# A two-layer hybrid decoder step on eight cores: token blocks of 384, 384 and 272 columns in place of 512, 512 and 16

## The chip, the cores and the metric

One Trainium2 chip with two dies of four cores. The kernel runs on all 8 cores, each with its own eighth of the tokens and with no exchange between cores. The metric is the device time of the slowest core in microseconds (us). TensorE (PE) does the matmuls, ScalarE (ACT) and VectorE (DVE) take the results out of PSUM, GpSimd (POOL) issues the weight loads and SyncE (SP) the other transfers.

## What is computed

Two layers over a prompt group (8 sequences of 2048 positions, one on each core) and a sample group (128 sequences of one position, 16 on each core). Cut to what matters:

```python
proj = x @ w_in                                   # u | v | bg | cg | xb | xc | gates
vn = layer_norm(v);  ha = u * (tril(W_s) @ vn + b_s)      # branch A, chunks of 128 positions
z = cg * xb;         hb = bg * conv3(z)                   # branch B, causal, depthwise
hc = (window_means(xc) - xc) @ w_pool * pool_scale        # branch C
merged = sum_i sigmoid(gate_i) * (branch_i @ w_proj_i)
h = layer_norm(ALPHA * x + merged @ w_o)
out = layer_norm(ALPHA * h + relu(h @ w_ff1)**2 @ w_ff2)
```

The model width is 1024, the inner width of the last line 4096. The samples have the convolution's and the pooling's past as inputs, and a spatial matrix that is only its first diagonal entry, so in branches A and B their 16 columns need other constants and another source than the prompt columns.

## The kernel before, in words

Each core does its 2048 prompt tokens in two passes of 1024, per layer: four steps (layer 0 pass 0, layer 0 pass 1, layer 1 pass 0, layer 1 pass 1). The 16 sample tokens ride in the steps of pass 0, as tile 8 behind the eight prompt tiles of 128 tokens (`has_s`, `NTI = 9`). So the first and the third step hold 1040 tokens, the second and the fourth 1024.

Two kinds of products alternate. In one kind the tokens are stationary and the weights stream, 512 columns at a time, by tiles of 128 tokens (`xstat_project`: v, xc, w_o and w_ff2). In the other kind the weights are stationary, 128 by 128, and the tokens stream from `T`, or from the branch buffer `hv` (that is `B2`), in blocks of a table `WT`: 512, 512 and 16 columns in the steps with samples, 512 and 512 in the others. One output block (j, w) is a group of 8 matmuls into one PSUM bank. These block loops are

- branch A's u (per 128 channels c: a group of 8 for u, then one small matmul per token tile against the spatial matrix `WsT` or, for the samples, `WsS`, then on DVE a multiply-add and a multiply),
- branch B (`b_conv` and the loop over cp ahead of `conv_rows_out`): three groups per block (cg, xb, bg), ACT copies cg out, DVE multiplies by xb into `zbuf`, ACT does the first tap, DVE the other two and the multiply by bg. The samples have their own buffer `zsb`,
- `merge_branch`, three times: a gate group and a projection group per block, run with a lag of two blocks,
- `ff1_group`: one group, ReLU on ACT, multiply on DVE. For the first quarter (gq = 0) the order is by block w, outer, and j, inner, so that the first block starts while the layer norm still delivers the last tiles of `T` (`ln1.to_T`, a transpose on PE and a copy on ACT). For the other quarters j is outer.

The order on each engine is the order in which the program text adds the operations (`Sched.add`); each operation waits on semaphores for the writers and readers of its buffers. PSUM has 8 banks, taken by the one that was taken longest ago (`bank1`, `bank2`), ftmp has 6 buffers, zbuf 3. The ring of weights has 10 slots, filled by POOL in program order as the slots come free. The sample columns of `T` lie right behind the prompt columns (columns 1024 to 1039), so 1040 columns are contiguous.

Of the kernel before, what the change touches and what calls it, by code (L numbers as in the profile page):

```python
# [170 lines left out]
def build_nc():  # L171
# [454 lines left out]
    for kstep, (l, p) in enumerate(steps):  # L626
        nxt = steps[kstep + 1] if kstep + 1 < len(steps) else None
        has_s = (p == 0)
        NTI = 9 if has_s else 8
# [72 lines left out]
        for cp in range(4):  # L702
            if has_s and kstep > 0 and cp == 1:
                sample_rows()
            if has_s and kstep > 0 and cp == 2:
                sample_rows_out()
            su = load_unit(w_in[l, :, C_U + cp * 256: C_U + (cp + 1) * 256])
            for cc in range(2):
                c = cp * 2 + cc
                g = c // 2  # L710
                for w, (t0, n) in enumerate(cur["WT"]):
                    bu = bank1()
                    pe_group([(pcols(bu, 0, n), ring[:, su, kc, cc * 128:(cc + 1) * 128], T[:, kc, t0:t0 + n],
                               kc == 0, kc == 7) for kc in range(8)],
                             [slotb[su]] + [Tb[i] for i in wt_tiles(w)], [bank[bu]])
# [2 lines left out]
                    if w < 2:
                        pe_group([(pcols(bs_, j * 128, 128), xh[:, 4 * w + j, c * 128:(c + 1) * 128],
                                   WsT[:, g, :], True, True) for j in range(4)],  # L720
                                 [XH[4 * w + j] for j in range(4)] + [lcst], [bank[bs_]])
                        dve_stt(ftmp[:, f, :].rearrange("p (j t) -> p j t", j=4),
                                pcols(bs_, 0, 512).rearrange("p (j t) -> p j t", j=4),
                                pv(l, PV_LNVG, c),
                                Bias2[:, c:c + 1, :].to_broadcast([128, 4, 128]),
                                ALU.mult, ALU.add, [bank[bs_], lcst, cst], [ftb[f]])
                    else:
                        pe_group([(pcols(bs_, 0, SP_), xh[:, 8, c * 128:(c + 1) * 128],
                                   WsS[:, g, :], True, True)], [XH[8], lcst], [bank[bs_]])
                        dve_stt(ftmp[:, f, 0:SP_], pcols(bs_, 0, SP_), pv(l, PV_LNVG, c),  # L730
                                Bias2s[:, c:c + 1].to_broadcast([128, SP_]),
                                ALU.mult, ALU.add, [bank[bs_], lcst, cst], [ftb[f]])
# [20 lines left out]

        for cp in range(4):
# [8 lines left out]
            for cc in range(2):  # L763
                c = cp * 2 + cc
                prev_z = None
                for w, (t0, n) in enumerate(cur["WT"]):
# [11 lines left out]
                    if w < 2:
                        zi = state["zb"] % 3
                        state["zb"] += 1  # L780
                        dve_tt(zbuf[:, zi, 2:2 + n], ftmp[:, f, 0:n], pcols(bxb, 0, n), ALU.mult,
                               [ftb[f], bank[bxb]], [zbb[zi]])
                        if w == 0:
                            if p == 0:
                                S.add("dve", lambda e, zi=zi: e.memset(zbuf[:, zi, 0:2], 0.0), (), [zbb[zi]])
                            else:
                                dve_copy(zbuf[:, zi, 0:2], zcar[:, c, :], [zcb], [zbb[zi]])
                        else:
                            dve_copy(zbuf[:, zi, 0:2], zbuf[:, prev_z, 512:514], [zbb[prev_z]], [zbb[zi]])
                            if p == 0:  # L790
                                dve_copy(zcar[:, c, :], zbuf[:, zi, 512:514], [zbb[zi]], [zcb])
                            else:
                                dve_copy(zsf[:, c, SP_:SP_ + 2], zbuf[:, zi, 512:514], [zbb[zi]], [zsfb])
                        prev_z = zi
                        item = (c, w, t0, n, (lambda k3, zi=zi, n=n: zbuf[:, zi, k3:k3 + n]), zbb[zi], f, bbg)
                    else:
                        dve_tt(zsb[:, c, :, 2], ftmp[:, f, 0:n], pcols(bxb, 0, n), ALU.mult,
                               [ftb[f], bank[bxb]], [zsbb])
# [310 lines left out]
```

How the kernel before makes its waits and increments, by code:

```python
        def run(engname, e):  # L100
            known = {}
            for op in sched.ops[engname]:
                deps = {}
                for k, v in op.raw.items():
                    if k == engname and engname == "pe":
                        continue
                    deps[k] = max(deps.get(k, -1), v)
                for k, v in op.other.items():
                    if k == engname:
                        continue
                    deps[k] = max(deps.get(k, -1), v)
                for k, v in deps.items():
                    if known.get(k, -1) >= v:
                        continue
                    e.wait_ge(sems[k], v)
                    known[k] = v
                ins = op.emit(e)
                if op.dma:
                    ins.then_inc(sems[op.tok[0]], 16)
                else:
                    ins.then_inc(sems[op.tok[0]], 1)
            if engname == "sp":
                for k, v in final_waits.items():
                    if known.get(k, -1) < v:
                        e.wait_ge(sems[k], v)
```

## Time and profile before

| | us |
|---|---|
| median of 3 runs (lowest to highest) | 2671.63 (2668.45 to 2672.88) |
| the profiled execution, its own time | 2672.26 |
| its span, slowest core (the eight: 2662.4 to 2670.7) | 2670.7 |
| PE busy, share of the span | 2564.7, 96% |
| DVE busy | 1201.4, 45% |
| ACT busy | 777.5, 29% |
| mean granted clock of PE on the eight cores | 0.986 to 0.989 |

The profile is of core 3, the slowest. Busy time is summed over the instructions of an engine; matmuls overlap, so a matmul's own duration is longer than the distance to the next one. Idle time of an engine stands with what ended it. The granted clock is a share of 2.4 GHz, and 0.5 of it is 1.2 GHz.

### The profile page before, as it was taken

The numbers are of one execution on the slowest core, as the hardware profiler recorded it, in microseconds if no ns is written. First come the engines' busy times: TensorE is split into PE (matmuls) and PEld (weight loads), VectorE is DVE, ScalarE is ACT, GpSimd is POOL, SyncE is SP. The second block draws the span as 40 slices with busy tenths as digits, with TensorE's granted clock in tenths as the row PEclk, the third lists the DMA queues.
The fourth block names the chain that finished last, engine by engine and source line by source line (L and its number), as shares of the span: only waits on it lengthen the run. The fifth ranks groups of instructions, "written<-read, shape, count | busy, mean of one in ns | idle before, by whom it ended". The sixth has DMA issues, their size and how long they took to land.

```text
span 2670.7 us, 40806 instructions; the slowest of 8 cores (2662.4 to 2670.7 us)
## 1 busy us (share of the span) xinstructions
PE 2564.7 (96%) x14756; PEld 1245.5 (47%) x14756; DVE 1201.4 (45%) x2135; ACT 777.5 (29%) x1471; POOL 266.1 (10%) x320
## 2 busy tenths in 40 slices
PE   6699999899999999999999999989999999999997
PEld 3344454444444445444445445544444444544443
DVE  2526415533572631643374452273337444146336
ACT  2122252411321215421151223351114122524112
POOL 1111000010011110111011100101001111000000
PEclk9799999999999999999999999999999999999999
DMA  8755545474695563559577463544747764464442
GB/s 152 127 71 65 75 61 72 60 99 64 123 172 70 74 86 43 76 69 127 80 179 108 62 87 49 82 62 72 103 73 169 92 80 68 58 87 67 63 69 74
DMA packets 312952, 231.81 MB, mean 87 GB/s; under 512 B 7602, under 2 KB 298674, under 8 KB 312724
## 3 DMA queue, kind: packets, MB, share of 16 engines
q0 software_dynamic: 299968, 186.26, 52.9%
q1 hardware_dynamic: 12788, 42.94, 5.0%
q8 instruction: 123, 2.02, 0.3%
q14 instruction: 73, 0.60, 0.1%
HBM read 397.51 MB, written 19.87 MB: 156 GB/s over the span
## 4 chain that ended last, share of the span: by engine, by line
PE 84%; DVE 7%; issue 4%; DMA 3%; ACT 2%; DVEq 0%; SPq 0%; ACTq 0%; POOLq 0%
PE ps L342 83%; DVE R L379 2%; DVE R L376 2%; DMA ring<-w_ff 1%; ACT T L362 1%; PE ps L350 1%; DMA R<-x_p 1%; DVE mv L371 0%; ACT B L362 0%; DMA maskt<-c_mask 0%; DVE sm L369 0%; DVE stat L646 0%; ACT sm L362 0%; DVE stat L647 0%; ACT xctm L362 0%
## 5 line engine op out<-in xcount | busy, mean ns | idle before, releaser
L342 PE MATMUL ps<-T,ring 128*128 128x512 bf16 (+1 forms) x7040 | 1314.6, 339 | 10.2 <-ACT T L362 8.6
L342 PEld LDWEIGHTS ps<-T,ring 128*128 128x128 bf16 x7040 | 591.6, 98 | 668.1 <-issue 27.7
L362 ACT ACTIVATE ftmp<-ps 128x512 f32<-128x512 f32 (+1 forms) x640 | 317.0, 513 | 1225.0 <-PE ps L342 1221.6
L342 PE MATMUL ps<-ring,B 128*128 128x512 bf16 x2720 | 598.6, 380 | 8.8 <-DVE sm L491 3.7
L365 DVE TENSOR_TENSOR B<-ftmp,ps 128x512 bf16<-128x512 f32 (+1 forms) x560 | 321.4, 583 | 480.7 <-ACT ftmp L362 278.7
L342 PEld LDWEIGHTS ps<-ring,B 128*128 128x128 bf16 x2720 | 263.4, 98 | 322.4 <-issue 16.2
L342 PE MATMUL ps<-B,ring 128*128 128x512 bf16 (+1 forms) x1920 | 375.4, 337 | 0.0
L365 DVE TENSOR_TENSOR ftmp<-ftmp,ps 128x512 f32<-128x512 f32 x160 | 93.4, 584 | 434.4 <-PE ps L342 434.4
L342 PEld LDWEIGHTS ps<-B,ring 128*128 128x128 bf16 x1920 | 163.0, 97 | 181.5
L342 PE MATMUL ps<-ring,T 128*128 128x512 bf16 x1088 | 241.5, 379 | 3.1 <-DVE mv L648 2.6
L321 POOL DMA_DIRECT2D ring<-w_in x128 | 112.7, 883 | 872.5 <-PE ps L342 841.2
L321 POOL DMA_DIRECT2D ring<-w_ff x96 | 84.2, 881 | 900.9 <-PE ps L342 728.1
L342 PEld LDWEIGHTS ps<-ring,T 128*128 128x128 bf16 x1088 | 105.0, 98 | 124.2 <-issue 4.5
L362 ACT ACTIVATE xctm<-R 128x1024 bf16<-128x1024 f32 x102 | 107.8, 1057 | 152.2 <-DVE sm L491 77.3
L365 DVE TENSOR_TENSOR R<-R,ps 128x1024 f32<-128x1024 f32 x68 | 83.0, 1221 | 153.3 <-PE ps L342 153.3
L379 DVE SCALAR_TENSOR_TENSOR ftmp<-zbuf,pvec_sb,ftmp 128x512 f32<-128x512 f32 x128 | 96.1, 751 | 62.6 <-ACT ftmp L362 55.6
L365 DVE TENSOR_TENSOR B<-B,ftmp 128x512 bf16<-128x512 bf16 x160 | 94.2, 589 | 17.2 <-DVE ftmp L365 0.7
L379 DVE SCALAR_TENSOR_TENSOR R<-stage,sm,lnbc_sb 128x1024 f32<-128x1024 f32 x68 | 87.3, 1284 | 7.8 <-DVE sm L491 0.9
L379 DVE SCALAR_TENSOR_TENSOR stage<-R,sm,lnbc_sb 128x1024 f32<-128x1024 f32 x68 | 87.3, 1284 | 7.8 <-DVE mv L371 1.6
L362 ACT ACTIVATE ftmp<-zbuf,pvec_sb 128x512 f32<-128x512 f32 x64 | 52.0, 813 | 127.5 <-DVE zbuf L383 104.7
L379 DVE SCALAR_TENSOR_TENSOR R<-R,ps 128x1024 f32<-128x1024 f32 x34 | 41.5, 1221 | 79.4 <-PE ps L342 79.4
L362 ACT ACTIVATE B<-ps,pvec_sb 128x128 bf16<-128x128 f32 (+1 forms) x272 | 72.5, 420 | 0.6 <-issue 0.6
(89 smaller groups left out, 972.0 us busy)
## 6 DMA issues: line engine op xcount, KB each, us to landing
ring<-w_in POOLq DMA_DIRECT2D x112, 512.0 KB, 8.6
ring<-w_ff POOLq DMA_DIRECT2D x64, 512.0 KB, 13.3
ring<-w_ff POOLq DMA_DIRECT2D x32, 1024.0 KB, 10.6
ring<-w_in POOLq DMA_DIRECT2D x16, 1024.0 KB, 10.1
hx<-R SPq DMA_DIRECT2D x17, 512.0 KB, 5.4
R<-hx SPq DMA_DIRECT2D x17, 512.0 KB, 4.8
R<-x_p SPq DMA_DIRECT2D x16, 512.0 KB, 13.0
ring<-w_proj_a POOLq DMA_DIRECT2D x16, 512.0 KB, 16.0
```

What stands on the lines that cost most here:

```text
L321: return S.add("pool", lambda e: e.dma_start(out=out, in_=in_), reads, writes, dma=True)
L342: ins = e.matmul(o, l, r, start=st, stop=sp_)
L350: ins = e.transpose(o, i, idn)
L362: return S.add("act", lambda e: e.activation(out=out, in_=in_, func=func, **kw), reads, writes)
L365: return S.add("dve", lambda e: e.tensor_tensor(out=out, in0=in0, in1=in1, op=op), reads, writes)
L376: return S.add("dve", lambda e: e.scalar_tensor_tensor(out=out, in0=in0, scalar=scalar, in1=in1, op0=op0, op1=op1, accum_out=accum_out), r ...
L379: return S.add("dve", lambda e: e.scalar_tensor_tensor(out=out, in0=in0, scalar=scalar, in1=in1, op0=op0, op1=op1), reads, writes)
```

## The change

The block table of the steps with samples becomes (0, 384), (384, 384), (768, 272), and the last block now has two prompt tiles (256 columns) and the samples (16 columns). The other steps keep 512 and 512. The code that told prompt from samples by the block's number now splits inside a block; `wt_tiles` and a new `w_of` give the tiles of a block and the block of a tile. In the start of the first quarter of w_ff1, the groups with j = 3 to 6 now stand ahead of the last `ln1.to_T` in steps with samples, where it was j = 3 and 4; in the other steps nothing moves.

```diff
-WT = [(0, 512), (512, 512), (PT, SP_)]
+WT_S = [(0, 384), (384, 384), (768, 256 + SP_)]
+WT_P = [(0, 512), (512, 512)]
...
     def wt_tiles(w):
-        return list(range(4 * w, 4 * w + 4)) if w < 2 else [8]
+        if cur["NTI"] == 9:
+            return list(range(3 * w, 3 * w + 3))
+        return list(range(4 * w, 4 * w + 4))
+
+    def w_of(i):
+        return i // 3 if cur["NTI"] == 9 else i // 4
...
-        cur["NTI"], cur["WT"] = NTI, (WT if has_s else WT[:2])
+        cur["NTI"], cur["WT"] = NTI, (WT_S if has_s else WT_P)
...
+                    tl = wt_tiles(w)
+                    np128 = len([i for i in tl if i < 8])
+                    mms = [(pcols(bs_, (i - tl[0]) * 128, 128), xh[:, i, c * 128:(c + 1) * 128], WsT[:, g, :],
+                            True, True) for i in tl if i < 8]
+                    if 8 in tl:
+                        mms.append((pcols(bs_, np128 * 128, SP_), xh[:, 8, c * 128:(c + 1) * 128], WsS[:, g, :],
+                                    True, True))
+                    pe_group(mms, [XH[i] for i in tl] + [lcst], [bank[bs_]])
...
+                    if 8 in tl:
+                        dve_stt(ftmp[:, f, np128 * 128:np128 * 128 + SP_], pcols(bs_, np128 * 128, SP_),
+                                pv(l, PV_LNVG, c), Bias2s[:, c:c + 1].to_broadcast([128, SP_]),
                                 ALU.mult, ALU.add, [bank[bs_], lcst, cst], [ftb[f]])
...
+        def b_conv(c, w, t0, n, parts, f, bbg):
+            for (a0, m, zsrc, zb_) in parts:
+                fa = ftmp[:, f, a0:a0 + m]
+                act(fa, zsrc(0), AF.Identity, [zb_, cst], [ftb[f]], bias=pv(l, PV_CB, c), scale=pv(l, PV_CW0, c))
+                for k3 in (1, 2):
+                    dve_stt(fa, zsrc(k3), pv(l, PV_CW0 + k3, c), fa, ALU.mult, ALU.add,
+                            [zb_, ftb[f], cst], [ftb[f]])
+            dve_tt(hv[:, c, t0:t0 + n], ftmp[:, f, 0:n], pcols(bbg, 0, n), ALU.mult,
+                   [ftb[f], bank[bbg]], [HB[(c, w)]])
...
+                    m = min(n, PT - t0)
...
+                    parts = [(0, m, (lambda k3, zi=zi, m=m: zbuf[:, zi, k3:k3 + m]), zbb[zi])]
+                    if m < n:
+                        dve_tt(zsb[:, c, :, 2], ftmp[:, f, m:n], pcols(bxb, m, n - m), ALU.mult,
                                [ftb[f], bank[bxb]], [zsbb])
                         dve_copy(zsf[:, c, 0:SP_], zsb[:, c, :, 2], [zsbb], [zsfb])
+                        parts.append((m, SP_, (lambda k3, c=c: zsb[:, c, :, k3]), zsbb))
+                    b_conv(c, w, t0, n, parts, f, bbg)
...
-        ff1_group(0, 3, 0, AG)
-        ff1_group(0, 4, 0, AG)
+        n1 = 7 if has_s else 5
+        for j in range(3, n1):
+            ff1_group(0, j, 0, AG)
         ln1.to_T(last)
-        for j in range(5, 8):
+        for j in range(n1, 8):
             ff1_group(0, j, 0, AG)
```

Where the order moves, in three places.

TensorE in the first `merge_branch` of the first step, before (`T,ring` is a gate group, `B,ring` a projection group):

```order
L342 MATMUL ps<-B,ring 128x512 x8
L342 MATMUL ps<-T,ring 128x512 x8
L342 MATMUL ps<-B,ring 128x512 x8
L342 MATMUL ps<-T,ring 128x512 x8
L342 MATMUL ps<-B,ring 128x16 x8
L342 MATMUL ps<-T,ring 128x16 x8
```

And now:

```order
L344 MATMUL ps<-B,ring 128x384 x8
L344 MATMUL ps<-T,ring 128x384 x8
L344 MATMUL ps<-B,ring 128x384 x8
L344 MATMUL ps<-T,ring 128x384 x8
L344 MATMUL ps<-B,ring 128x272 x8
L344 MATMUL ps<-T,ring 128x272 x8
```

The number and the order of the groups stay, only their widths move; the same holds for branch B and the later quarters of w_ff1.

VectorE in branch B of the first step, one c (128 channels), before:

```order
L365 TENSOR_TENSOR zbuf<-ftmp,ps 128x512
L785 MEMSET zbuf 128x2
L379 SCALAR_TENSOR_TENSOR ftmp<-zbuf,pvec_sb,ftmp 128x512 x2
L365 TENSOR_TENSOR B<-ftmp,ps 128x512
L365 TENSOR_TENSOR zbuf<-ftmp,ps 128x512
L383 COPY zbuf<-zbuf 128x2
L383 COPY zcar<-zbuf 128x2
L379 SCALAR_TENSOR_TENSOR ftmp<-zbuf,pvec_sb,ftmp 128x512 x2
L365 TENSOR_TENSOR B<-ftmp,ps 128x512
L365 TENSOR_TENSOR zsb<-ftmp,ps 128x16
L383 COPY zsf<-zsb 128x16
L379 SCALAR_TENSOR_TENSOR ftmp<-zsb,pvec_sb,ftmp 128x16 x2
```

And now, its third block alone:

```order
L367 TENSOR_TENSOR zbuf<-ftmp,ps 128x256
L385 COPY zbuf<-zbuf 128x2
L385 COPY zcar<-zbuf 128x2
L367 TENSOR_TENSOR zsb<-ftmp,ps 128x16
L385 COPY zsf<-zsb 128x16
L381 SCALAR_TENSOR_TENSOR ftmp<-zbuf,pvec_sb,ftmp 128x256 x2
L381 SCALAR_TENSOR_TENSOR ftmp<-zsb,pvec_sb,ftmp 128x16 x2
L367 TENSOR_TENSOR B<-ftmp,ps 128x272
```

The third block now has a prompt part and a sample part, four instructions more on DVE per c (the multiply into zbuf, the copy of the two columns before it, two taps) and one more on ACT.

TensorE at the start of the first quarter of w_ff1 in the first step (`identb,xctm` are the transposes of `ln1.to_T`, the last of them tile 8), before:

```order
L342 MATMUL ps<-T,ring 128x512 x8
L350 MATMUL ps<-identb,xctm 128x128 x8
L342 MATMUL ps<-T,ring 128x512 x16
L350 MATMUL ps<-identb,xctm 128x128 x8
L342 MATMUL ps<-T,ring 128x512 x16
L350 MATMUL ps<-identb,xctm 128x128 x8
L342 MATMUL ps<-T,ring 128x512 x88
L342 MATMUL ps<-T,ring 128x16 x64
```

And now:

```order
L344 MATMUL ps<-T,ring 128x384 x8
L352 MATMUL ps<-identb,xctm 128x128 x8
L344 MATMUL ps<-T,ring 128x384 x16
L352 MATMUL ps<-identb,xctm 128x128 x8
L344 MATMUL ps<-T,ring 128x384 x32
L352 MATMUL ps<-identb,xctm 128x128 x8
L344 MATMUL ps<-T,ring 128x384 x72
L344 MATMUL ps<-T,ring 128x272 x64
```

Two more groups stand ahead of the last transposes, and the 64 matmuls of the last block are 272 wide.

## Rows read from the trace of the kernel before

**Rows 1.** The page's head and its first part.
```profile
span 2670.7 us, 40806 instructions; the slowest of 8 cores (2662.4 to 2670.7 us)
PE 2564.7 (96%) x14756; PEld 1245.5 (47%) x14756; DVE 1201.4 (45%) x2135; ACT 777.5 (29%) x1471; POOL 266.1 (10%) x320
```
**Rows 2.** Groups by shape, matmuls and weight loads: count, busy us, mean ns, idle before.
```profile
L342 PE MATMUL ps<-T,ring 128*128 128x512 bf16 x5632 | 1281.7, 382 | 9.6 <-ACT T L362 8.6 <-DVE ftmp L379 0.9
...
L342 PE MATMUL ps<-T,ring 128*128 128x16 bf16 x1408 | 54.6, 169 | 0.7 <-DVE B L365 0.7
...
L350 PE MATMUL ps<-identb,xctm 128*128 128x128 bf16 x272 | 21.6, 224 | 11.1 <-ACT xctm L362 11.1
...
L342 PE MATMUL ps<-B,ring 128*128 128x16 bf16 x384 | 16.7, 169 | 0.0
```
**Rows 3.** Timeline, PE, a merge of step 1: start, duration, what, [idle before].
```profile
395.28 0.35 PE L342 MATMUL ps<-B,ring 128*128 128x16 bf16 x8
395.69 1.89 PE L342 MATMUL ps<-B,ring 128*128 128x512 bf16 x8
...
402.59 0.35 PE L342 MATMUL ps<-B,ring 128*128 128x16 bf16 x8
```
**Rows 4.** Groups by shape, DVE and ACT in the block loops.
```profile
L365 DVE TENSOR_TENSOR B<-ftmp,ps 128x512 bf16<-128x512 f32 x448 | 307.5, 687 | 458.7 <-ACT ftmp L362 278.5 <-PE ps L342 160.2 <-DVE ftmp L379 12.8
...
L379 DVE SCALAR_TENSOR_TENSOR ftmp<-zbuf,pvec_sb,ftmp 128x512 f32<-128x512 f32 x128 | 96.1, 751 | 62.6 <-ACT ftmp L362 55.6 <-DVE ftmp L379 0.5
...
L362 ACT ACTIVATE ftmp<-zbuf,pvec_sb 128x512 f32<-128x512 f32 x64 | 52.0, 813 | 127.5 <-DVE zbuf L383 104.7 <-DVE zbuf L785 22.7
...
L365 DVE TENSOR_TENSOR B<-ftmp,ps 128x16 bf16<-128x16 f32 x112 | 18.2, 167 | 22.0 <-PE ps L342 19.9 <-ACT ftmp L362 0.2
...
L379 DVE SCALAR_TENSOR_TENSOR ftmp<-zsb,pvec_sb,ftmp 128x16 f32<-128x16 f32 x32 | 7.5, 235 | 5.7 <-ACT ftmp L362 3.9 <-DVE ftmp L379 0.2
...
L362 ACT ACTIVATE ftmp<-zsb,pvec_sb 128x16 f32<-128x16 f32 x16 | 6.5, 407 | 37.5 <-DVE zsb L365 37.5
```
**Rows 5.** Timeline, DVE, one c of branch B in step 3.
```profile
1558.14 0.69 DVE L365 TENSOR_TENSOR zbuf<-ftmp,ps 128x512 f32<-128x512 f32 x1
...
1563.24 0.69 DVE L365 TENSOR_TENSOR zbuf<-ftmp,ps 128x512 f32<-128x512 f32 x1 [0.91 <-PE ps L342]
...
1567.40 0.17 DVE L365 TENSOR_TENSOR zsb<-ftmp,ps 128x16 f32<-128x16 f32 x1
...
1568.18 0.58 DVE L379 SCALAR_TENSOR_TENSOR ftmp<-zsb,pvec_sb,ftmp 128x16 f32<-128x16 f32 x2 [0.33 <-ACT ftmp L362]
...
1569.11 0.69 DVE L365 TENSOR_TENSOR zbuf<-ftmp,ps 128x512 f32<-128x512 f32 x1
```
**Rows 6.** Timeline, PE, start of the first quarter of w_ff1 in step 1.
```profile
478.83 1.89 PE L342 MATMUL ps<-T,ring 128*128 128x512 bf16 x8
...
482.27 0.61 PE L350 MATMUL ps<-identb,xctm 128*128 128x128 bf16 x8 [1.55 <-ACT xctm L362]
...
486.65 0.61 PE L350 MATMUL ps<-identb,xctm 128*128 128x128 bf16 x8 [0.32 <-ACT xctm L362]
487.09 3.62 PE L342 MATMUL ps<-T,ring 128*128 128x512 bf16 x16
494.55 0.61 PE L350 MATMUL ps<-identb,xctm 128*128 128x128 bf16 x8 [3.84 <-ACT xctm L362]
```
**Rows 7.** Timeline, PE, end of that quarter.
```profile
517.59 0.34 PE L342 MATMUL ps<-T,ring 128*128 128x16 bf16 x8 [0.37 <-DVE B L365]
518.23 2.38 PE L342 MATMUL ps<-ring,B 128*128 128x512 bf16 x7 [0.30 <-DVE B L365]
```
**Rows 8.** Windows: busy of PE, PEld, DVE, ACT, POOL, then granted clock, DMA share, GB/s.
```profile
494.50:500.00 5.50, 5.45 (x24) 2.45 (x25) 2.66 (x4) 3.79 (x6) 0.00 (x0) 0.69 0.52 70
518.20:525.00 6.80, 6.77 (x24) 2.81 (x25) 1.43 (x3) 0.07 (x1) 1.20 (x2) 0.75 0.89 82
1794.50:1800.00 5.50, 5.48 (x24) 2.47 (x25) 2.66 (x4) 3.77 (x6) 0.00 (x0) 0.69 0.02 4
```

More of the change, by code:

```diff
@@ L717, in build_nc @@
                     f = ft_next()
[L718 to L731, printed above, removed]
+                    tl = wt_tiles(w)
[6 more added lines that the diff above has]
+                    pe_group(mms, [XH[i] for i in tl] + [lcst], [bank[bs_]])
+                    dve_stt(ftmp[:, f, 0:np128 * 128].rearrange("p (j t) -> p j t", j=np128),
+                            pcols(bs_, 0, np128 * 128).rearrange("p (j t) -> p j t", j=np128),
+                            pv(l, PV_LNVG, c),
+                            Bias2[:, c:c + 1, :].to_broadcast([128, np128, 128]),
+                            ALU.mult, ALU.add, [bank[bs_], lcst, cst], [ftb[f]])
+                    if 8 in tl:
+                        dve_stt(ftmp[:, f, np128 * 128:np128 * 128 + SP_], pcols(bs_, np128 * 128, SP_),
+                                pv(l, PV_LNVG, c), Bias2s[:, c:c + 1].to_broadcast([128, SP_]),
                                 ALU.mult, ALU.add, [bank[bs_], lcst, cst], [ftb[f]])
@@ L777, in build_nc @@
                     act(ftmp[:, f, 0:n], pcols(bcg, 0, n), AF.Copy, [bank[bcg]], [ftb[f]])
[L778 to L787, printed above, removed]
-                        else:
[L789 to L797, printed above, removed]
@@ new lines, in build_nc @@
+                    m = min(n, PT - t0)
+                    zi = state["zb"] % 3
+                    state["zb"] += 1
+                    dve_tt(zbuf[:, zi, 2:2 + m], ftmp[:, f, 0:m], pcols(bxb, 0, m), ALU.mult,
+                           [ftb[f], bank[bxb]], [zbb[zi]])
+                    if w > 0:
+                        zp, mp = prev_z
+                        dve_copy(zbuf[:, zi, 0:2], zbuf[:, zp, mp:mp + 2], [zbb[zp]], [zbb[zi]])
+                    elif p == 0:
+                        S.add("dve", lambda e, zi=zi: e.memset(zbuf[:, zi, 0:2], 0.0), (), [zbb[zi]])
+                    else:
+                        dve_copy(zbuf[:, zi, 0:2], zcar[:, c, :], [zcb], [zbb[zi]])
@@ new lines, in build_nc @@
+                    if t0 + m == PT:
+                        if p == 0:
+                            dve_copy(zcar[:, c, :], zbuf[:, zi, m:m + 2], [zbb[zi]], [zcb])
+                        else:
+                            dve_copy(zsf[:, c, SP_:SP_ + 2], zbuf[:, zi, m:m + 2], [zbb[zi]], [zsfb])
+                    prev_z = (zi, m)
+                    parts = [(0, m, (lambda k3, zi=zi, m=m: zbuf[:, zi, k3:k3 + m]), zbb[zi])]
+                    if m < n:
+                        dve_tt(zsb[:, c, :, 2], ftmp[:, f, m:n], pcols(bxb, m, n - m), ALU.mult,
@@ L902, in c_lin @@
             pe_group(mms, [Dtb[di], slotb[swp]], [bank[bh], bank[bh + 1]])
-            w = i // 4 if i < NT128 else 2
+            w = w_of(i)
             for dj in range(8):
@@ L915, in wo @@
             c0, n = tile_cols(i)
-            w = i // 4 if i < NT128 else 2
+            w = w_of(i)
             b = xstat_project(i, wslots, [MG[(j, w)] for j in range(8)], lambda kc, c0=c0: mg[:, kc, c0:c0 + 128])
@@ L1000, in ff2 @@
                 c0, n = tile_cols(i)
-                w = i // 4 if i < NT128 else 2
+                w = w_of(i)
                 b = xstat_project(i, slots, [AG[(j, w)] for j in range(8)], lambda kc, c0=c0: av[:, kc, c0:c0 + 128])
```

11 lines of the change are left out of this document (1 added, 10 removed).

## The prediction

> **What bounds the kernel now.** I read the page's head first: TensorE is busy for 96% of the span, VectorE for 45% [rows 1], so what a change is worth is what it takes from TensorE's own row of matmuls, unless it makes TensorE wait. Then the groups by shape: the 512-column matmuls carry the time and hardly wait (9.6 us of idle ahead of 5632 of them), and there are 1408 + 384 = 1792 matmuls of 16 columns in the two steps with samples [rows 2]. Then TensorE's timeline in a merge, for the distance between matmuls, since a matmul's own duration (382 ns, 169 ns) overlaps the next: two groups of 16-column matmuls take 395.69 - 395.28 = 0.41 us, that is about 25.2 ns a matmul with the shared drain left out, and the whole cycle of six groups takes 402.59 - 395.28 = 7.31 us [rows 3]. Last, the places in which the 1040-column blocks meet a wait: branch B on VectorE [rows 5] and the start and end of the first quarter of w_ff1 [rows 6 to 8].
>
> **Term 1, the matmuls.** Their number stays (three groups of 8 per block row, before and after), their columns too (1040). Only widths move. The cycle of 7.31 us holds 32 matmuls of 512 and 16 of 16 columns: (7310 - 16 x 25.2) / 32 = 215.9 ns for 512. For 128 columns, a burst of eight takes 0.61 us [rows 6] with 224 ns for the last one [rows 2]: (610 - 224) / 7 = 55.1 ns. Between them lies a line of (215.9 - 55.1) / 384 = 0.419 ns a column with 1.5 ns to spare at zero, which is 2.4 GHz. The 16-column matmul would cost 8 ns on it and costs 25: that is the waste. Neither 384 nor 272 columns occur in the trace. Bounds: from below the line, 162.3 and 115.4 ns; it is interpolation between two measured widths, and at 128 columns nothing else shows. Then three matmuls cost 2 x 162.3 + 115.4 = 440.0 ns, where they cost 2 x 215.9 + 25.2 = 457.0 ns, 17.0 ns less; times 1792 it is **30.4 us**. With the 55.1 ns wrong by 1 ns it is 29 to 32. From above: a straight line through 16 and 512 columns (0.384 ns a column), which gives 166.6 and 123.5 ns and a sum of 457, nothing gained. I take the line through 128, for it is the nearer width to 272 and it alone agrees with the slope of 2.4 GHz.
>
> The Trainium skill ("TensorE: Matmul & The Clock Gate", section "Back-to-back issue gap") speaks against this change: in a real stream of weight loads and matmuls it gives some 81 ns at 128 columns and some 131 ns at 512, and by any such single line three matmuls with 1040 columns cost the same however they are split, so term 1 would be zero. The trace does not agree (55.1 and 215.9 ns). The same section's table also has a least distance of about 25 ns for small matmuls, and there the trace agrees (25.2 ns).
>
> **Term 2, the start and the end of the first quarter of w_ff1 (twice).** TensorE waits there for the layer norm's last tile: 1.55, 0.32 and 3.84 us [rows 6]. That chain (w_o result, norm and transposes through VectorE and ScalarE) doesn't depend on the blocks, but two ReLUs and two multiplies of the first groups stand in it in order; each is 128 columns shorter, about 0.11 us on ScalarE and 0.13 us on VectorE (1.05 ns a column [rows 4]), together 0.48 us, so the last transposes can start at 494.07 and not 494.55. By then TensorE has done five groups of 1.727 us (8.63 us) before, and now seven of 1.298 us (9.09 us): 0.46 us more. So 0.94 us a step; the three waits become about 1.98, 1.2 and 1.8 us. At the end the 64 matmuls of 16 columns go faster than ScalarE and VectorE can empty the banks, which costs 0.37 + 0.30 us [rows 7] plus drains, about 0.75 us; with 272 columns a group takes 0.92 us and its two readers about 0.4 us each, so that goes. (0.94 + 0.75) x 2 = **3.4 us**.
>
> **Term 3, the clock.** After the 3.84 us wait the granted clock is 0.69 over 5.5 us, in both steps, and after the small matmuls of the first step 0.75 over 6.8 us [rows 8]; full speed is 1.0, the dips go to 1.2 GHz. Each costs (1 - 0.69) x 5.5 = 1.7 us. The third has no more small matmuls ahead of it. The first two follow a wait that is halved to 1.8 us; the wait of 1.55 us [rows 6] was followed by no dip. I take all three as gone, **5.2 us**, and from 1.7 us as the other bound; dips elsewhere may come or go by 1.7 us each.
>
> **Term 4, VectorE in branch B: nothing, but with thin cover.** One c takes 1569.11 - 1558.14 = 10.97 us, in which VectorE waits for TensorE only once, 0.91 us [rows 5]; the rest, 10.06 us, is one chain of its own work and ScalarE's tap in the middle. Per column the chain costs two multiplies (1.05 ns each), two taps (1.04) and ScalarE's tap (0.82) [rows 4], 5.0 ns, and the columns stay 1040. A prompt block of 512 takes 1567.40 - 1563.24 = 4.16 us [rows 5], so 4.16 - 2.56 = 1.60 us of it are fixed. The third block now has a prompt part: plus 1.60 us fixed. Of the sample part some 0.6 us are saved, since its first multiply and copy run under ScalarE's prompt tap and its last multiply joins the 272-wide one. The sample tap on ScalarE waits for VectorE's prompt taps (same ftmp buffer) and stays exposed. So the chain is about **11.1 us** per c, against 3 x (16 x 162.3 + 8 x 115.4) = 10.56 us on TensorE: VectorE becomes the slower one in this loop and falls behind by 0.5 us per c, 4.3 us over eight. What hides it is the eight banks: a group waits for the reader of the eighth group before it, that is, the second group of a block waits for the end of the chain three blocks earlier. For the last block that comes at 10.56 x 7 + 7.79 + 0.92 = 82.6 us after the loop's start, and the chain of three blocks before ends at 2.6 + 0.5 + 7 x 11.1 = 80.8 us. Cover 1.8 us. Behind the loop, the projection of the third block needs the last result: seven groups, 84.5 + 8.7 = 93.2 us, against 91.9. Cover 1.3 us. The backlog is then worked off in the merge, where VectorE needs about 3.1 us in 7.
>
> **The rest costs nothing.** The u loop gets one more VectorE instruction of about 0.2 us per c: some 3.5 of 4.0 us, hidden. The other loops have the same instructions on 1040 columns. POOL and SP issue the same transfers in the same order; TensorE waits for none of them behind the first 100 us, and they are asked for at a 3.5% faster pace in half of the program. The steps without samples don't change.
>
> **Sum.** 30.4 + 3.4 + 5.2 = 39.0 us from the execution's own 2672.26 us is 2633.3 us. The median of the runs stands 0.6 us below that execution; so **2633 us**, 1.4% less.
>
> **The rivals.**
> - *Branch B becomes bound by VectorE's chain.* Same place, but the banks don't hold the lag, because the chain is longer than 11.1 us or the lag starts earlier. For it: cover of under 2 us on an estimate of eight instructions. Against: only the excess beyond the cover counts. If the loop ran wholly at 11.1 us it would give back 16 x 0.54 = 8.6 us: 2642 us; at 11.4 us, 13.4 us: 2646 us.
> - *The dips of the clock stay* or others come: 3.5 us back, 2636.5 us; two more elsewhere, 2640 us.
> - *A fixed cost at any width* (the line through 16 and 512 columns): term 1 is zero and the sum is 2672.3 - 8.6 = 2663.7 us, with the dips kept 2668 or so, within 0.2%. Against it stand the 55.1 ns at 128. The skill's rule of a single line, above, is this case.
> - *Slower: the weight load shows.* A load lasts about 98 ns and a 512-column matmul covers it amply; under 272 columns (115 ns) the cover is thin. If each matmul behind a 272-wide one were held up by 25.2 ns, the least distance seen, it would be 1792 x 25.2 = 45.2 us: 2633 + 45 = 2678 us, slower. It decides from (39.0 - 5.3) / 1792 = 19 ns on for less than 0.2% gain, from 22 ns for a loss. Against: at 16 and at 128 columns, with the same loads, the distances are 25 and 55 ns.
> - *The change doesn't do what it says*: the order shows 384 and 272 columns on every block loop, so no.
>
> **Numbers.** A measurement of this kernel can tell about 0.2% (5.3 us) from no change. Chances: the forecast with its dips either way (2628 to 2640) 0.76, branch B bound 0.16, fixed cost at any width 0.03 (half of it within 0.2%), slower 0.02, faster than 2628 0.03. The range from 2627 to 2647 us leaves out some 0.1. Faster by over 0.2%: 0.96; within 0.2%: 0.02; slower: 0.02.
>
> **What would show it.** Merges: a cycle of six groups in 7.04 us in place of 7.31; matmuls of 384 and 272 columns 162 and 115 ns apart. Branch B: VectorE without a wait for TensorE, blocks three per 11.1 us, TensorE at 10.56 us per c with at most a short wait at the last c; if TensorE waits for VectorE there in many places, the first rival holds. First quarter of w_ff1: last wait about 1.8 us, no idle of TensorE at its end, granted clock 1.0 behind both. It is wrong if the cycle of a merge isn't below 7.2 us.

## The result, and the profile after

The changed kernel takes 2635.7 us, median of 17 runs (the kernel before, in the same rounds: 2672.4 us), a ratio of 0.9872 with a 95% interval of 0.9849 to 0.9894: 1.3% less. The forecast was 2633 us in a range from 2627 to 2647 us. Ratios, and the times given for the runs below, leave out the runs in which the cores of one die or of both had a lower granted clock, but the ratio above still holds three of the changed kernel, at 2656 to 2660 us with cores 4 and 5 at a clock of 0.978, and without them it is 0.986, 1.4% less.

The page's head of the changed kernel, and its first part (core 1, the slowest):

```profile
span 2632.7 us, 40970 instructions; the slowest of 8 cores (2627.3 to 2632.7 us)
...
PE 2529.3 (96%) x14756; PEld 1373.7 (52%) x14756; DVE 1214.5 (46%) x2215; ACT 791.8 (30%) x1487; POOL 266.3 (10%) x320
```

TensorE has the same 14756 matmuls as in [rows 1] and is busy for 35.4 us less; the span is 38.0 us shorter. VectorE has 80 instructions more and ScalarE 16.

Groups by shape, which answer to [rows 2] (count, busy us, mean ns of one, idle before):

```profile
L344 PE MATMUL ps<-T,ring 128*128 128x384 bf16 x2816 | 491.6, 327 | 1.4 <-DVE B L367 1.0
...
L344 PE MATMUL ps<-T,ring 128*128 128x272 bf16 x1408 | 184.9, 279 | 1.9 <-DVE B L367 1.3 <-ACT B L364 0.7
```

TensorE's timeline in a merge of the first step, which answers to [rows 3] (start, duration, what):

```profile
396.42 1.09 PE L344 MATMUL ps<-B,ring 128*128 128x272 bf16 x8
...
398.27 1.46 PE L344 MATMUL ps<-B,ring 128*128 128x384 bf16 x8
399.57 1.46 PE L344 MATMUL ps<-T,ring 128*128 128x384 bf16 x8
...
403.47 1.09 PE L344 MATMUL ps<-B,ring 128*128 128x272 bf16 x8
```

The cycle of six groups is 403.47 - 396.42 = 7.05 us, where it was 7.31 us. A matmul of 384 columns stands (399.57 - 398.27) / 8 = 162.5 ns from the next, one of 272 columns (398.27 - 396.42) / 16 = 115.6 ns.

VectorE's timeline in branch B, one c of the third step, which answers to [rows 5]:

```profile
1482.72 0.55 DVE L367 TENSOR_TENSOR zbuf<-ftmp,ps 128x384 f32<-128x384 f32 x1
...
1486.19 0.55 DVE L367 TENSOR_TENSOR zbuf<-ftmp,ps 128x384 f32<-128x384 f32 x1
...
1489.71 0.41 DVE L367 TENSOR_TENSOR zbuf<-ftmp,ps 128x256 f32<-128x256 f32 x1
...
1491.54 1.07 DVE L381 SCALAR_TENSOR_TENSOR ftmp<-zbuf,pvec_sb,ftmp 128x256 f32<-128x256 f32 x2 [0.52 <-ACT ftmp L364]
1493.22 0.57 DVE L381 SCALAR_TENSOR_TENSOR ftmp<-zsb,pvec_sb,ftmp 128x16 f32<-128x16 f32 x2 [0.61 <-ACT ftmp L364]
...
1494.32 0.55 DVE L367 TENSOR_TENSOR zbuf<-ftmp,ps 128x384 f32<-128x384 f32 x1
```

In this c no instruction waits for TensorE any more; apart from waits of 0.17 us behind VectorE's own taps, all are for ScalarE's tap. One c takes 1494.32 - 1482.72 = 11.60 us, more than TensorE's 10.56. Over the loop the c differ: 11.4 us in the shortest, 11.8 us in the longest, 11.6 us in the mean of both steps. And TensorE now waits for VectorE at the end of this loop. Its timeline at the end of branch B in the third step:

```profile
1540.58 11.05 PE L344 MATMUL ps<-T,ring 128*128 128x272 bf16 x72 [0.21 <-DVE B L367]
1551.99 3.31 PE L344 MATMUL ps<-T,ring 128*128 128x272 bf16 x24 [0.36 <-DVE B L367]
1555.46 2.39 PE L344 MATMUL ps<-T,ring 128*128 128x384 bf16 x16 [0.15 <-DVE B L367]
...
1563.41 1.09 PE L344 MATMUL ps<-B,ring 128*128 128x272 bf16 x8 [0.36 <-DVE B L367]
```

That is 1.08 us in the step, 0.36 us of it in the merge behind the loop; the first step has 1.04 us.

TensorE's timeline at the start of the first quarter of w_ff1 in the first step, which answers to [rows 6], and its end, which answers to [rows 7]:

```profile
472.62 1.46 PE L344 MATMUL ps<-T,ring 128*128 128x384 bf16 x8
475.71 0.61 PE L352 MATMUL ps<-identb,xctm 128*128 128x128 bf16 x8 [1.63 <-ACT xctm L364]
...
480.09 0.61 PE L352 MATMUL ps<-identb,xctm 128*128 128x128 bf16 x8 [1.17 <-ACT xctm L364]
480.54 5.36 PE L344 MATMUL ps<-T,ring 128*128 128x384 bf16 x32
487.52 0.61 PE L352 MATMUL ps<-identb,xctm 128*128 128x128 bf16 x8 [1.62 <-ACT xctm L364]
487.96 19.28 PE L344 MATMUL ps<-T,ring 128*128 128x384 bf16 x136
507.08 13.11 PE L344 MATMUL ps<-ring,B 128*128 128x512 bf16 x60
```

The waits are 1.63, 1.17 and 1.62 us (1.55, 0.32 and 3.84 before), there is no wait at the end, and from the first group to w_ff2 it takes 507.08 - 472.62 = 34.46 us (39.40 before). The windows behind these two places and behind the same start in the third step, which answer to [rows 8] (busy of PE, PEld, DVE, ACT, POOL, then granted clock, DMA share, GB/s):

```profile
487.50:493.00 5.50, 5.48 (x39) 3.50 (x40) 3.68 (x8) 4.88 (x10) 0.00 (x0) 1.00 0.26 36
505.50:512.00 6.50, 6.50 (x39) 3.58 (x37) 2.62 (x5) 1.19 (x3) 0.88 (x1) 1.00 1.17 129
1766.80:1772.30 5.50, 5.46 (x39) 3.51 (x40) 3.67 (x8) 4.89 (x10) 0.00 (x0) 1.00 0.12 16
```

The granted clock is 1.00 in all three, where it was 0.69, 0.75 and 0.69. Over the eight cores the mean granted clock rose from 0.986 to 0.989 before to 0.988 to 0.990.

### The profile page after: what moved, and what is told of

Its sections match the earlier page's. It is cut to its first block, busy times and chain, and to the rows that moved or that the text cites. A ratio compares the mean times of both kernels' runs of the same rounds, so it can differ in the third digit from the quotient of the medians.

```text
span 2632.7 us, 40970 instructions; the slowest of 8 cores (2627.3 to 2632.7 us)
## 1 busy us (share of the span) xinstructions
PE 2529.3 (96%) x14756; PEld 1373.7 (52%) x14756; DVE 1214.5 (46%) x2215; ACT 791.8 (30%) x1487; POOL 266.3 (10%) x320
## 4 chain that ended last, share of the span: by engine, by line
PE 83%; DVE 8%; issue 4%; ACT 3%; DMA 1%; DVEq 0%; SPq 0%; ACTq 0%
PE ps L344 82%; DVE R L381 2%; DVE R L378 2%; DVE ftmp L381 1%; ACT T L364 1%; PE ps L352 1%; ACT ftmp L364 1%; DMA R<-x_p 1%; DVE mv L373 0%; ACT B L364 0%; DVE zbuf L367 0%; DVE sm L371 0%; DMA maskt<-c_mask 0%; DVEq L116 0%; DVE stat L652 0%
## 5 line engine op out<-in xcount | busy, mean ns | idle before, releaser
L344 PE MATMUL ps<-T,ring 128*128 128x384 bf16 (+2 forms) x7040 | 1289.4, 339 | 12.0 <-ACT T L364 8.6
L344 PEld LDWEIGHTS ps<-T,ring 128*128 128x128 bf16 x7040 | 685.4, 98 | 544.5 <-issue 23.1
L364 ACT ACTIVATE ftmp<-ps 128x384 f32<-128x384 f32 (+2 forms) x640 | 327.5, 517 | 1145.3 <-PE ps L344 794.3
L367 DVE TENSOR_TENSOR B<-ftmp,ps 128x512 bf16<-128x512 f32 (+2 forms) x560 | 326.4, 584 | 458.1 <-ACT ftmp L364 256.9
L344 PE MATMUL ps<-B,ring 128*128 128x384 bf16 (+2 forms) x1920 | 370.3, 338 | 0.7 <-DVE B L367 0.7
L367 DVE TENSOR_TENSOR ftmp<-ftmp,ps 128x384 f32<-128x384 f32 (+1 forms) x160 | 93.5, 584 | 413.5 <-PE ps L344 413.2
L344 PEld LDWEIGHTS ps<-B,ring 128*128 128x128 bf16 x1920 | 187.7, 98 | 148.4 <-issue 1.4
L381 DVE SCALAR_TENSOR_TENSOR ftmp<-zbuf,pvec_sb,ftmp 128x384 f32<-128x384 f32 (+2 forms) x160 | 103.2, 645 | 73.4 <-ACT ftmp L364 65.1
L364 ACT ACTIVATE ftmp<-zbuf,pvec_sb 128x384 f32<-128x384 f32 (+2 forms) x80 | 58.5, 731 | 176.9 <-DVE zbuf L385 110.5
L367 DVE TENSOR_TENSOR B<-B,ftmp 128x384 bf16<-128x384 bf16 (+1 forms) x160 | 94.2, 589 | 16.7
```

Source lines behind the costliest of these rows:

```text
L344: ins = e.matmul(o, l, r, start=st, stop=sp_)
L364: return S.add("act", lambda e: e.activation(out=out, in_=in_, func=func, **kw), reads, writes)
L367: return S.add("dve", lambda e: e.tensor_tensor(out=out, in0=in0, in1=in1, op=op), reads, writes)
L381: return S.add("dve", lambda e: e.scalar_tensor_tensor(out=out, in0=in0, scalar=scalar, in1=in1, op0=op0, op1=op1), reads, writes)
```

## Experiments

Each ran beside the kernel before. "The changed kernel" is 2635 us in a second set of runs too:

> The changed kernel once more, as the yardstick on the same chip as the next three: 2635.7 us, 0.986 to 0.987 of the kernel before.

Measured: 0.9862 (0.9845 to 0.988) of the kernel before, 2634.7 us.

**The price of a 16-column matmul, by leaving them out.**

```diff
     def pe_group(mms, reads, writes):
+        if len(mms) == 8 and mms[0][2].shape[-1] == SP_ and mms[-1][4] and not mms[0][4]:
+            mms = [mms[0][:4] + (True,)]
```

> The kernel before; each group of eight 16-column matmuls is cut to its first one, so the sample columns get only an eighth of their sums in u, branch B, the gates, the projections and w_ff1. It leaves out 7/8 of 1792 = 1568 matmuls. Theory (25.2 ns each): 39.5 us less, 2633 us, some 1 to 3 us lower if the waits and the dip at the end of the first quarter go too. Rival, that a 16-column matmul costs the 8 ns of the line through 128 and 512 columns: 12.5 us less, 2660 us.

Measured: 0.9884 (0.9866 to 0.9902), 2642 us, so 31 us less and not 39.5. TensorE's timeline in a merge of this run:

```profile
387.98 0.17 PE L344 MATMUL ps<-B,ring 128*128 128x16 bf16 x1
388.01 0.17 PE L344 MATMUL ps<-T,ring 128*128 128x16 bf16 x1
388.03 1.89 PE L344 MATMUL ps<-B,ring 128*128 128x512 bf16 x8
...
394.94 0.17 PE L344 MATMUL ps<-B,ring 128*128 128x16 bf16 x1
```

The cycle is 394.94 - 387.98 = 6.96 us against 7.31 us, 0.35 us for 14 matmuls left out, 25 ns each: the price stands where the loop has no wait, and the 8 ns of the rival are excluded. The rest of the 39.5 us came back as waits. With so short a third group the engines that empty the banks are late at the end of the first quarter of w_ff1:

```profile
507.83 0.17 PE L344 MATMUL ps<-T,ring 128*128 128x16 bf16 x1 [1.56 <-DVE B L367]
508.47 11.77 PE L344 MATMUL ps<-ring,B 128*128 128x512 bf16 x46 [0.47 <-DVE B L367]
```

(0.37 and 0.30 us in [rows 7]), and the dips of the granted clock, summed over the profile from 100 to 2620 us (what the clock lacks to 1.0, times the length), come to 20.1 us in this run where they come to 17.1 us in the kernel before. These two account for some 6 of the 8.5 us. Of the rest, TensorE's table of waits shows 1.1 us for a copy of ScalarE into T that the kernel before never waits for, and 1.1 us more without a releaser; what remains is not traced.

**Another split of the same columns.**

```diff
-WT_S = [(0, 384), (384, 384), (768, 256 + SP_)]
+WT_S = [(0, 512), (512, 256), (768, 256 + SP_)]
...
-            return list(range(3 * w, 3 * w + 3))
+            return [[0, 1, 2, 3], [4, 5], [6, 7, 8]][w]
```

> The changed kernel with blocks of 512, 256 and 272 columns. Theory (a matmul costs 0.419 ns a column and 1.5 ns, at any width above the floor of 25 ns): 215.9 + 108.7 + 115.4 = 440.0 ns for three, the same as with 384, 384 and 272, so the merges' cycle stays 7.05 us. The first blocks of w_ff1 being wider, the waits there fall from 4.4 to 2.4 us a step: 2636 - 4 = 2632 us. Rival, a step in the cost between 256 and 384 columns: the cycle of a merge differs from 7.05 us; 5 ns a matmul would be 9 us.

Measured: 0.9856 (0.984 to 0.9871), 2634 us. A merge's timeline:

```profile
394.95 1.04 PE L344 MATMUL ps<-B,ring 128*128 128x256 bf16 x8
...
396.70 1.09 PE L344 MATMUL ps<-B,ring 128*128 128x272 bf16 x8
...
403.75 1.09 PE L344 MATMUL ps<-B,ring 128*128 128x272 bf16 x8
```

The cycle is 7.05 us, as with 384, 384 and 272, and 256 columns cost (396.70 - 394.95) / 16 = 109.4 ns. So the distances at 128, 256, 272, 384 and 512 columns (55.1, 109.4, 115.6, 162.5 and 215.9 ns) lie on one line to within 1 ns, and the rival's step between 256 and 384 columns isn't there. The 4.4 us of waits at the start of w_ff1 went as expected (TensorE waits for the transposes' source 4.4 us in the whole run and not 8.8), but its waits for VectorE's results rose from 4.0 us in the changed kernel's profile to 5.6 us. Of the 4 us forecast some 2 are left, no more than these runs can tell, so there is no version to prefer.

**The order at the start of w_ff1, taken apart from the widths.** First the new widths with the old order:

```diff
-        n1 = 7 if has_s else 5
+        n1 = 5
```

> The changed kernel with only j = 3 and 4 ahead of the last transposes of the first quarter of w_ff1 in all steps, as before the change. Theory: the five groups of 384 columns fill 2.6 us less than seven, so TensorE's last wait there is 1.6 + 2.6 = 4.2 us in both steps with samples and the granted clock dips behind it again: 5.2 us of wait and up to 3.4 us of clock over the changed kernel's 2635.7, so 2641 to 2644 us. Rival, that the place of the two groups does not matter since the wait is made up for later: 2636 us.

Measured: 0.9888 (0.9872 to 0.9903), 2642.7 us. TensorE's timeline in the first step, and the windows behind the last transposes of the first step and around those of the third:

```profile
487.27 0.61 PE L352 MATMUL ps<-identb,xctm 128*128 128x128 bf16 x8 [4.21 <-ACT xctm L364]
```

```profile
488.00:493.50 5.50, 5.50 (x26) 2.84 (x24) 2.35 (x5) 3.07 (x6) 0.00 (x0) 0.69 0.10 13
1766.00:1772.00 6.00, 1.79 (x12) 1.29 (x12) 2.99 (x6) 3.72 (x7) 0.00 (x0) 0.68 1.17 160
```

The wait is 4.21 us (4.2 expected), in the third step too. The clock dips are back in both steps and on all eight cores. In the third step the dip on this core begins 2.1 us before the wait ends (the second window holds most of that wait: TensorE is busy for 1.79 us of 6), so part of it falls into idle time. The kernel loses some 7 us. Then the old widths with the new order:

```diff
-        ff1_group(0, 3, 0, AG)
-        ff1_group(0, 4, 0, AG)
+        n1 = 7 if has_s else 5
+        for j in range(3, n1):
+            ff1_group(0, j, 0, AG)
         ln1.to_T(last)
-        for j in range(5, 8):
+        for j in range(n1, 8):
             ff1_group(0, j, 0, AG)
```

> The kernel before, with blocks of 512, 512 and 16, and only the groups j = 5 and 6 moved ahead of the last transposes in steps with samples. Theory: the wait of 3.84 us shrinks to 0.4 us and the clock stays up behind it: 6.9 + 3.4 = 10.3 us less than 2672.4, so 2662 us; with the dips kept 2665.5. Rival, that the wait only moves to the banks or to a later block: 2672 us.

Measured: 0.9952 (0.9939 to 0.9964), 2660 us, 12.8 us less than before. Its waits for the layer norm's last tiles are these (TensorE's waits: us in total, times, longest):

```profile
PE ps L350 <- ACT xctm L362: 4.2, 6, 1.6
```

4.2 us, where the kernel before has 11.1; 6.9 us as expected. The window behind the last transposes of the first step is at full clock:

```profile
495.00:500.50 5.50, 5.47 (x32) 2.79 (x33) 3.86 (x7) 5.13 (x9) 0.00 (x0) 1.00 0.44 59
```

On all eight cores the dips behind these transposes are gone, in both steps. In the profiled cores all dips together come to 12.3 us and not 17.1, 4.8 us less, and with the 6.9 us that is 11.7 of the 11.9 us by which the span is shorter. So a third of the whole gain (12.8 of 37 us) is to be had by this order alone, without any new width.

**VectorE's chain in branch B, shorter and longer.** Shorter: both of ScalarE's taps are issued ahead of VectorE's, with a tag of its own for the sample columns of ftmp.

```diff
+            fbs = [ftb[f], ftsb[f]][:len(parts)]
-            for (a0, m, zsrc, zb_) in parts:
+            for (a0, m, zsrc, zb_), fb in zip(parts, fbs):
                 fa = ftmp[:, f, a0:a0 + m]
-                act(fa, zsrc(0), AF.Identity, [zb_, cst], [ftb[f]], bias=pv(l, PV_CB, c), scale=pv(l, PV_CW0, c))
+                act(fa, zsrc(0), AF.Identity, [zb_, cst], [fb], bias=pv(l, PV_CB, c), scale=pv(l, PV_CW0, c))
+            for (a0, m, zsrc, zb_), fb in zip(parts, fbs):
+                fa = ftmp[:, f, a0:a0 + m]
                 for k3 in (1, 2):
                     dve_stt(fa, zsrc(k3), pv(l, PV_CW0 + k3, c), fa, ALU.mult, ALU.add,
-                            [zb_, ftb[f], cst], [ftb[f]])
+                            [zb_, fb, cst], [fb])
...
-                   [ftb[f], bank[bbg]], [HB[(c, w)]])
+                   fbs + [bank[bbg]], [HB[(c, w)]])
```

> The changed kernel; in branch B both taps of ScalarE (256 prompt columns and 16 sample columns) are issued ahead of VectorE's taps, with a tag of its own for the sample part of ftmp, so the sample tap no longer waits for VectorE's prompt taps. Theory: the chain per c falls from 11.6 us by the exposed tap, 0.6 us, to 11.0 us, VectorE's lag at the end of the loop from 8.3 to 3.5 us, and TensorE's waits for VectorE there (about 1 us a step) go: 2634 us. Rival, that these waits have another cause: they stay, 2636 us.

Measured: 0.9856 (0.9835 to 0.9877), 2633.0 us, 1.7 us under the changed kernel of the same set, less than these runs can tell. The trace tells it. VectorE's timeline of this run:

```profile
1491.99 0.55 DVE L368 TENSOR_TENSOR zbuf<-ftmp,ps 128x384 f32<-128x384 f32 x1
...
1500.61 1.07 DVE L382 SCALAR_TENSOR_TENSOR ftmp<-zbuf,pvec_sb,ftmp 128x256 f32<-128x256 f32 x2 [0.52 <-ACT ftmp L365]
1501.60 0.57 DVE L382 SCALAR_TENSOR_TENSOR ftmp<-zsb,pvec_sb,ftmp 128x16 f32<-128x16 f32 x2
...
1502.70 0.55 DVE L368 TENSOR_TENSOR zbuf<-ftmp,ps 128x384 f32<-128x384 f32 x1
```

The sample taps follow without a wait. One c takes 10.71 us here, as in the shortest c of the loop, where the shortest of the changed kernel take 11.41 us; the means are 10.9 and 11.6 us. None of TensorE's waits in branch B is left.

What made the chain 11.6 us and not the forecast 11.1 us? The third block of the c shown above takes 1494.32 - 1489.71 = 4.61 us, where the working had 4.1. In the changed kernel's trace ScalarE's prompt tap of such a block starts 0.61 us after the copy into zbuf that it needs (VectorE's and ScalarE's timelines, the third block of the last c):

```profile
1559.08 0.16 DVE L385 COPY zbuf<-zbuf 128x2 f32<-128x2 f32 x1
```

```profile
1559.69 0.60 ACT L364 ACTIVATE ftmp<-zbuf,pvec_sb 128x256 f32<-128x256 f32 x1 [2.74 <-DVE zsb L367]
```

Its releaser is VectorE's multiply into zsb, which reads other columns of the same ftmp buffer. One tag stands for the whole buffer, so the tap waits for a reader that it doesn't touch. The next run gives the sample columns a tag of their own, and leaves the taps in the changed kernel's order:

```diff
-                    act(ftmp[:, f, 0:n], pcols(bcg, 0, n), AF.Copy, [bank[bcg]], [ftb[f]])
+                    act(ftmp[:, f, 0:n], pcols(bcg, 0, n), AF.Copy, [bank[bcg]],
+                        [ftb[f], ftsb[f]] if m < n else [ftb[f]])
...
                         dve_tt(zsb[:, c, :, 2], ftmp[:, f, m:n], pcols(bxb, m, n - m), ALU.mult,
-                               [ftb[f], bank[bxb]], [zsbb])
+                               [ftsb[f], bank[bxb]], [zsbb])
```

> The changed kernel; the sample columns of ftmp have a tag of their own for ScalarE's copy of cg and VectorE's multiply into zsb, nothing else moves. In the changed kernel's trace ScalarE's prompt tap of the third block starts 0.61 us after the copy into zbuf, released by VectorE's multiply into zsb, where the taps of the other blocks start 0.26 us after it. Theory: that wait is a false one by the shared tag and makes most of the 0.5 us by which the chain of 11.6 us exceeds the forecast 11.1: the tap starts 0.26 us after the copy, the chain falls to 11.2 or 11.3 us, VectorE's lag to 5.1 to 6 us, under the 7 us that the banks hold, so TensorE's waits in branch B go: 2633 us. Rival, that the tap is late for another reason (ScalarE's queue): it stays at 0.6 us and the chain at 11.6.

Measured: 0.9854 (0.9811 to 0.9896), 2633.6 us. Its timelines, VectorE and then ScalarE:

```profile
1481.08 0.55 DVE L368 TENSOR_TENSOR zbuf<-ftmp,ps 128x384 f32<-128x384 f32 x1
...
1484.55 0.55 DVE L368 TENSOR_TENSOR zbuf<-ftmp,ps 128x384 f32<-128x384 f32 x1
...
1488.06 0.42 DVE L368 TENSOR_TENSOR zbuf<-ftmp,ps 128x256 f32<-128x256 f32 x1
...
1492.13 0.55 DVE L368 TENSOR_TENSOR zbuf<-ftmp,ps 128x384 f32<-128x384 f32 x1
...
1499.44 0.16 DVE L386 COPY zbuf<-zbuf 128x2 f32<-128x2 f32 x1
```

```profile
1499.69 0.60 ACT L365 ACTIVATE ftmp<-zbuf,pvec_sb 128x256 f32<-128x256 f32 x1 [2.40 <-DVE zbuf L386]
```

The tap starts 0.25 us behind the copy, the third block takes 4.07 us, the chain of this c 3.47 + 3.51 + 4.07 = 11.05 us, and TensorE has no wait in branch B. The shortest c went from 11.41 to 11.04 us, by just the 0.61 - 0.25 = 0.36 us of the tap, and the mean from 11.6 to 11.2 us. So the shared tag made 0.36 of the half microsecond; the rest is that in each of these kernels single c take up to 0.4 to 0.6 us longer than the shortest (in the c shown above two small instructions of VectorE last 0.41 and 0.33 us in place of 0.17). The time can't be told from that of the run with the taps ahead; the trace, not the time, decides here.

Longer: one more pass over 384 columns of zbuf per c.

```diff
+                    if has_s and w == 0:
+                        dve_tt(zbuf[:, zi, 2:2 + m], zbuf[:, zi, 2:2 + m], zbuf[:, zi, 2:2 + m], ALU.max,
+                               [zbb[zi]], [zbb[zi]])
```

> The changed kernel with one more multiply-like pass of 384 columns on VectorE per c in branch B (the larger of zbuf and itself, which changes nothing), in steps with samples: the chain per c grows from 11.6 by 0.65 to 12.3 us. Theory: the banks' cover is used up, so all of it counts: 16 x 0.65 = 10.4 us more, 2646 us, and the loop runs at VectorE's pace in its last c. Rival, that the banks and the merge behind still take it up: under 3 us more, 2636 to 2639 us.

Measured: 0.9904 (0.9888 to 0.992), 2645.4 us, 10.7 us over the changed kernel. TensorE's timeline:

```profile
243.05 7.59 PE L344 MATMUL ps<-T,ring 128*128 128x384 bf16 x48 [0.81 <-DVE B L367]
250.99 3.31 PE L344 MATMUL ps<-T,ring 128*128 128x272 bf16 x24 [0.35 <-DVE B L367]
255.12 7.59 PE L344 MATMUL ps<-T,ring 128*128 128x384 bf16 x48 [0.81 <-DVE B L367]
```

From the middle of the loop on TensorE's period is VectorE's, 255.12 - 243.05 = 12.07 us, with some 1.17 us of waits per c; the first step's nine waits sum to 5.05 us and the third step's to 4.99 us. Four runs give one picture of the cover. With the mean length of a c in both steps, the lag that VectorE gathers over the eight c, less what TensorE waits, is 8 x (12.1 - 10.56) - 5.0 = 7.3 us here and 8 x (11.6 - 10.56) - 1.1 = 7.2 us in the changed kernel, while lags of 8 x (11.2 - 10.56) = 5.1 us with the sample tag and of 2.7 us with the taps ahead cost no wait. The banks and the merge behind take up some 7 us of lag, and what goes beyond it stands in TensorE's waits. Those grew by 10.0 - 2.1 = 7.9 us over the changed kernel's, so that of the 10.7 us by which this run is longer some 3 us lie elsewhere; that the time is as forecast (10.4 us) is in part luck.

**Taps ahead, and more groups ahead of the last transposes in all steps.** The edit is that of the run with the taps ahead, and `n1 = 8 if has_s else 7`.

> The changed kernel with the taps ahead as in the run with that name, and in the first quarter of w_ff1 all eight groups of the first block ahead of the last transposes in steps with samples, seven in the others. Theory: 2 us from branch B; the last wait falls from 1.6 to 0.3 us in the two steps with samples (2.6 us) and from 3.84 to 0.4 us in the two others (6.9 us), whose dips of the clock (1.7 us each) go too: 15 us, 2621 us. Rival, that in steps without samples the late copy of tile 7 then stops the second block, which needs it: 2 us back each, 2625 us.

Measured: 0.9842 (0.9826 to 0.9858), 2628.9 us, the fastest version here, some 6 us under the changed kernel and not 15. In steps with samples the last wait fell to 0.42 and 0.60 us, but the next group then waits 0.39 us for its bank. In the steps without samples nothing moved, since the wait there is another one than I had taken it for. TensorE's timeline of this run in the second step, and ScalarE's, the fourth copy into T of that norm:

```profile
1109.54 3.57 PE L345 MATMUL ps<-T,ring 128*128 128x512 bf16 x8 [4.32 <-ACT T L365]
```

```profile
1108.39 1.00 ACT L365 ACTIVATE T<-ps 128x1024 bf16<-128x1024 bf16 x1
```

It is the first group of w_ff1 itself that waits 4.32 us for ScalarE's copy into T: its block of 512 columns needs tile 3, whose copy stands behind the norm's work in ScalarE's order. What stands ahead of the last transposes doesn't matter there. The kernel before waits there for the same, 4.31 us. The expectation rested on an assumption about a step that I hadn't looked up in the trace; its 6.9 us of wait and 3.4 us of clock did not come.

## Why the prediction was right, step by step

- *Term 1, the matmuls*: 30.4 us forecast. The cycle gives (7.31 - 7.05) / 16 = 16.3 ns for each of the 1792 triples, 29 us. (The rows give 0.41 us for sixteen matmuls of 16 columns, 25.6 ns and not 25.2; the 512 columns then cost 215.6 ns and the triple the same 457 ns, so term 1 doesn't hang on it.) The line through 128 and 512 columns was the right choice of the two bounds: 162.3 and 115.4 ns forecast, 162.5 and 115.6 measured, and 256 columns lie on it too (109.4). In the run with the new widths and the old order the kernel gains 30 us. The rule of the Trainium skill that went against the change ("TensorE: Matmul & The Clock Gate", section "Back-to-back issue gap", 81 ns at 128 and 131 ns at 512 columns in a stream of loads and matmuls) doesn't hold in any run here: they show 55 and 216 ns. The same section's least distance of about 25 ns does: leaving such matmuls out gave 25 ns for each.
- *Term 2, the first quarter of w_ff1*: without the clock the forecast for one step is 1.09 (term 1's share, 64 triples) + 0.94 + 0.75 = 2.78 us. Measured are 39.40 - 34.46 = 4.94 us in the first step and 4.82 us in the third, 1.7 us of each the dip of the clock, so 3.2 and 3.1 us. The three waits were forecast as 1.98, 1.2 and 1.8 us and are 1.63, 1.17 and 1.62 us. What I hadn't said is how much hangs on the moved groups: without them the last wait is 4.21 us.
- *Term 3, the clock*: all three dips are gone. By the mean clock of the eight cores (0.9875 before, 0.9891 after) the gain is (1 - 0.9875) x 2667 - (1 - 0.9891) x 2630 = 4.7 us. But 5.2 us were forecast for the slowest core, and there dips that the forecast didn't name went too: over the two profiles they come to 17.1 us before and 9.4 us after, 7.7 us less.
- *Term 4, branch B*: forecast nothing, with a chain of 11.1 us and cover of 1.8 us in the loop and 1.3 us behind it. The chain is 11.6 us in the mean and TensorE waits 1.06 us a step, 2.1 us in all. The step that failed is the one that let the sample part's first multiply "run under ScalarE's prompt tap": by the shared tag the tap waits for it, 0.36 us per c. With the tag split the chain is 11.04 us in the shortest c and 11.2 us in the mean, and the waits are gone, as forecast. The cover came out larger than forecast, some 7 us of lag by the four runs where the prediction had 4.3 + 1.3 = 5.6 us. The mechanism (VectorE falls behind, the banks hold it for the length of the loop) was right, and of the first rival, 8.6 us or more for a loop wholly at VectorE's pace, a quarter came.
- *The rivals*: fixed cost at any width and a weight load that shows are both excluded by the distances above. Under 272 columns the load, 98 ns, is still hidden.
- *The rest*: as forecast, but for one wait of 0.3 us for a transfer of w_ff in the kernel before, where the prediction had none.
- *Sum*: 39.0 us forecast from the execution's own time, 38.0 us measured by the spans. Term 1 fell short by some 1 us and branch B took 2.1 us; term 2 gave 0.9 us more and the clock of the slowest core 2.5 us more. These sum to 39.1 us; the remaining 1 us is not traced. So the mechanism of the main term is shown, while the closeness of the sum owes something to luck: dips that weren't forecast gave back what branch B took.

The gain has two halves that the change mixed: the new widths alone bring it to 2642.7 us (30 us), the order alone to 2660 us (12.8 us), both to 2635 us (37 us). They don't add up to 42.8 us, since the two moved groups fill less when they are narrower: the last wait falls by 4.21 - 1.62 = 2.59 us a step with 384 columns and by 3.45 us with 512, and the dips, in the mean of the eight cores, by 3.0 us (12.0 to 9.1) and by 3.9 us (14.0 to 10.1).

## What to carry to other kernels

A tail block of a few columns costs the least distance of a matmul, here 25 ns for 16 columns where a column is worth 0.42 ns; spread the tail over the other blocks where the count of groups stays the same. The two splits tried here cost TensorE the same per matmul. What does matter is what each block needs and frees: look up which tile the first block waits for, and fill a known wait with groups that don't need it. When two parts of one buffer come to be written by different work, give each its tag, or a false wait lengthens the chain. Where another engine's chain becomes longer than TensorE's loop, work out how much lag the banks hold over the length of the loop: here some 7 us cost nothing, and the lag beyond them came back as waits.

## What the runs showed that I had not expected

At the start of w_ff1, over the eight cores and both steps with samples, a dip of the granted clock came with 15 of 16 waits of 3.84 us (kernel before) and with all 16 of 4.21 us (new widths, old order), and with none of the waits of 1.6 us in the changed kernel and in the old widths with the new order. A dip costs about 1.7 us, nearly half as much again as the wait. So shortening that wait by 3.45 us in each of two steps brought 12.8 us and not 6.9: two such dips went, and in the slowest core more elsewhere. In the steps without samples the wait of 4.3 us before w_ff1 comes with a dip on every core, before and after the change, and that wait still stands. And leaving out 1568 matmuls of 25 ns brought 31 us, where replacing 1792 of them by a finer split of the same columns, which leaves no work out, brought 30: less work on TensorE in too short a group turns into waits for the engines behind it.
